# Sixteen element-wise transfers in DRAM in place of sixteen TensorE transposes of the key weights

## The chip, the cores and the metric

The kernel runs on one core of one Trainium2 chip. The metric is the device time of one execution in microseconds (us), lower is better. Engines are named as in the profile: PE is TensorE's matmul stream, PEld its weight loads, DVE is VectorE, ACT ScalarE, POOL GpSimd and SP SyncE. SP computes nothing: it issues transfers. A "q" behind an engine's name (SPq, ACTq) is that engine's sequencer, on which the issue of a transfer shows.

## The reference, cut to what matters

One decoder layer: RMSNorm, one input projection whose columns are split between two groups, an output projection with residual, and a last RMSNorm. Group A is a gated linear recurrence (eight blocks of 128 channels). Group B is attention with a small indexer that keeps 256 keys for each query. Its keys live in a shared latent `c` of 256 channels, and each of 8 heads has its own key weights `w_uk`:

```python
q_abs = jnp.einsum('bshd,hdc->bshc', q, w_uk)          # w_uk: 8 heads x 128 (d) x 256 (c), float32
...
logits = jnp.einsum('bqhc,bqkc->bqhk', qa_b, c_sel).astype(jnp.float32) * (HEAD_DIM ** -0.5)
```

The kernel uses the same product the other way: it makes each head's keys from the latent, keys = (w_uk turned) x c. For that TensorE needs `w_uk` with c, not d, over the 128 partitions: sixteen blocks (8 heads x 2 halves of c) of 128x128 float32 numbers, each turned. All of them together are 1 MB, 262,144 numbers.

## The kernel before, in words

Nearly every product is made in split precision: a float32 matrix is cut into a high and a low part and three matmuls are added (low x high, high x low, high x high). The program is written by hand for each engine, with semaphores, and each engine runs its own list strictly in order.

The stages are: loading and normalising x (turned by TensorE); tiles 0 to 2 of the input projection; the indexer, tiles 3 to 10; the recurrent stage, tiles 11 to 26, two for each of its eight blocks g; the attention's projections, tiles 27 to 42, two for each head h; the attention; the output projection.

A tile t of the projection goes in four pieces j. SP loads piece `w_raw` (256 KB) once the piece before it in the same place is used up (semaphore `w_lo_s`), POOL scales it (L809), ACT cuts the high part `w_hi` (function `high`, L903, which waits for PE to be done with the old piece, `w_used`), POOL makes the low part `w_lo` (L811), and PE runs 24 matmuls on it (`project_tile`, L1211 to L1213). There is one buffer per piece, so while PE works on piece j of tile t, piece j - 1 of tile t + 1 is made.

In the recurrent stage ACT's list for block g is (function `lru`): the two tiles' pieces, the first tap of the convolution `xc` (L1009), the high part of the gate weights (L1013), `xc_hi` (L1015), four pieces of the next tile, then the sigmoids, exp and root on the gates. PE's list is: both tiles, then `pe.wait_ge(gates_lo_s, g + 1)` and twelve matmuls of the gates (L1358 to L1360) on `xc_hi` and on `xc_lo`, which DVE makes (L1747). The first block's part of ACT's list begins after the indexer's last score (`ix_acc`).

The key weights: after the last recurrent block and the loads of tiles 27 and 28, SP loads `wuk` (L617, 1 MB, d over the partitions). PE turns it in sixteen transposes (L1376) after tile 28 and leaves the result in PSUM (`X[0]`, `X[1]`). ACT cuts the high parts (L1062), DVE the low ones (L1785), SP stores both to DRAM (L626), from where the attention loads each head's pair. Behind `wuk` on SP's list stand the stores of the last recurrent block (L594, L596) and the weights of the next tiles (L528).

Of the kernel before, what the change touches and what calls it, by code (L numbers as in the profile page):

```python
# [22 lines left out]
F32 = mybir.dt.float32  # L23
# [3 lines left out]
ACT = mybir.ActivationFunctionType  # L27
# [3 lines left out]
P = 128  # L31
# [5 lines left out]
G = LRU // P  # L37
CONV = 4
NH = 8
HD = 128  # L40
PAIRS = NH // 2
C = 256
CT = C // P
# [78 lines left out]
def layer(nc, a, out):  # L122
# [5 lines left out]
    ql_d = nc.dram_tensor("q_lo_dram", [NH, P, S], F32).ap()  # L128
    gate_d = nc.dram_tensor("gate_dram", [NH, P, S], F32).ap()
    c_d = nc.dram_tensor("c_dram", [CT, P, S], F32).ap()  # L130
    wkh_d = nc.dram_tensor("wuk_hi_dram", [NH, P, CT, HD], F32).ap()
    wkl_d = nc.dram_tensor("wuk_lo_dram", [NH, P, CT, HD], F32).ap()
    wvh_d = nc.dram_tensor("wuv_hi_dram", [PAIRS, P, CT, 2, HD], F32).ap()
# [5 lines left out]
    with ctx:  # L139
        def sem(name):  # L140
            return ctx.enter_context(nc.semaphore(name))

        def alloc(stack):
            return lambda name, shape, dt=F32: stack.enter_context(nc.sbuf_tensor(name, shape, dt))
# [11 lines left out]
        ident = sb("ident", [P, P])  # L156
# [44 lines left out]
        pu = ExitStack()  # L201
# [4 lines left out]
        pu = ExitStack()  # L206
# [3 lines left out]
        pu = ExitStack()  # L210
        cs_hi = alloc(pu)("cs_hi", [P, S], F32R)
        pu.close()
        pu = ExitStack()
# [17 lines left out]
        pu = ExitStack()  # L231
        y_hi = alloc(pu)("y_hi", [P, S], F32R)
        pu.close()
        pu = ExitStack()
# [3 lines left out]
        pu = ExitStack()  # L238
        xc_lo = alloc(pu)("xc_lo", [P, S], F32R)
        pu.close()  # L240
        pu = ExitStack()
# [4 lines left out]
        pu = ExitStack()  # L246
# [4 lines left out]
        pu = ExitStack()  # L251
        wuv = alloc(pu)("wuv", [P, PAIRS, CT, 2, HD])
        pu.close()
        pu = ExitStack()
# [3 lines left out]
        pu = ExitStack()  # L258
# [3 lines left out]
        pu = ExitStack()  # L262
# [3 lines left out]
        w_gates = sC("w_gates", [P, 2, P])  # L266
        mask_at = 4 * (3 * PIECES * PK * P + SCORED + 6 * S + 2 * P)
        pu = ExitStack()
        wuk = alloc(pu)("wuk", [P, NH, C])
        pu.close()  # L270
        pu = ExitStack()
        sU = alloc(pu)
# [3 lines left out]
        pu = ExitStack()  # L276
        wuv_hi = alloc(pu)("wuv_hi", [P, PAIRS, CT, 2, HD], F32R)
        pu.close()
        wuk_hi, wuk_lo = [wk0_hi, wk1_hi], [wk0_lo, wk1_lo]
# [10 lines left out]
        pu = ExitStack()  # L290
# [54 lines left out]
        PJ, X = PS[0:2], PS[2:4]  # L345
# [19 lines left out]
        bias_cp = sem("bias_cp")  # L365
        bias_st = sem("bias_st")
        wuk_in = sem("wuk_in")
        wuk_tp = sem("wuk_tp")
        wuk_hi_s = sem("wuk_hi_s")
        wuk_lo_s = sem("wuk_lo_s")  # L370
        wuk_st = [sem("wuk_st0"), sem("wuk_st1")]
# [58 lines left out]
        i_sig = sem("i_sig")  # L430
# [92 lines left out]
        def _(sp):  # L523
# [68 lines left out]
            def y_stores(g):  # L592
                sp.wait_ge(y_hi_s, g + 1)
                sp.dma_start(yh_d[ds(g, 1)].rearrange("o p s -> (o p) s"), y_hi[:, :].bitcast(F32)).then_inc(y_hi_st, 16)  # L594
                sp.wait_ge(y_lo_s, g + 1)
                sp.dma_start(yl_d[ds(g, 1)].rearrange("o p s -> (o p) s"), y_lo[:, :].bitcast(F32)).then_inc(y_lo_st, 16)  # L596
# [6 lines left out]
            def att_loads(h):  # L603
                weights(T_ATT + 2 * h, COL_Q + h * P)
                weights(T_ATT + 1 + 2 * h, COL_GB + h * P)
# [8 lines left out]
                sp.dma_start(gate_d[ds(h, 1)].rearrange("o p s -> (o p) s"), ig[:, :]).then_inc(gate_st, 16)  # L614

            att_loads(0)
            sp.dma_start(wuk[:, :, :], a["w_uk"][0].rearrange("h d c -> d h c")).then_inc(wuk_in, 16)  # L617
            y_stores(G - 1)

            att_loads(1)  # L620
# [244 lines left out]
        def _(act):  # L865
# [32 lines left out]
            def high(t, js=range(PIECES)):  # L898

                for j in js:  # L900
                    act.wait_ge(w_g_s, 4 * t + j - 3)
                    act.wait_ge(w_used, 4 * t + j + 1)
                    nc.scalar.activation(w_hi[:, j, :, :], w_raw[:, j, :, :], ACT.Copy).then_inc(w_hi_s, 1)  # L903
# [94 lines left out]
            def high_y(g):  # L998
                act.wait_ge(y_lru, g + 2)
                nc.scalar.activation(y_hi[:, :], sg[:, :], ACT.Copy).then_inc(y_hi_s, 1)  # L1000

            def lru(g, first=False):
                par = lambda k: lru_p[:, k, ds(g, 1)]
                if not first:
                    high(g * 2 + (T_LRU + 1), range(2))
                    high_y(g - 1)
                    high(g * 2 + (T_LRU + 1), range(2, PIECES))
                act.wait_ge(w_used, g * 8 + done(T_LRU))
                nc.scalar.activation(xc[:, :], PJ[1][:, :], ACT.Identity, scale=conv_w[:, CONV - 1, ds(g, 1)],  # L1009
                                     bias=par(0)).then_inc(xc0, 1)  # L1010

                act.wait_ge(gw_in, g * 32 + 32)
                nc.scalar.activation(wg_hi[:, :, :], w_gates[:, :, :], ACT.Copy).then_inc(wg_hi_s, 1)  # L1013
                act.wait_ge(pj_free[1], g + T_LRU // 2 + 2)
                nc.scalar.activation(xc_hi[:, :], xc[:, :], ACT.Copy).then_inc(xc_hi_s, 1)  # L1015
                high(g * 2 + (T_LRU + 2))
                act.wait_ge(gates_mm, g + 2)
                act.wait_ge(y_hi_st, 16 * g + 16)
                nc.scalar.activation(rg[:, :], X[0][:, :], ACT.Sigmoid, bias=par(1)).then_inc(r_sig, 1)
                nc.scalar.activation(ig[:, :], X[1][:, :], ACT.Sigmoid, bias=par(2)).then_inc(i_sig, 1)  # L1020
                act.wait_ge(y_lo_st, 16 * g + 16)
                nc.scalar.activation(sg[:, :], PJ[0][:, :], ACT.Sigmoid).then_inc(g_sig, 1)
                act.wait_ge(r_sig, g + 1)

                nc.scalar.activation(th[:, :], rg[:, :], ACT.Tanh, scale=decay[:, 0, ds(g, 1)])
                s = step.did(nc.scalar.activation(av[:, :], rg[:, :], ACT.Exp, scale=decay[:, 1, ds(g, 1)]))
                act.wait_ge(act_step, s)
                nc.scalar.activation(rg[:, :], av[:, :], ACT.Square).then_inc(a_sq, 1)
                act.wait_ge(one_m, g + 1)
                nc.scalar.activation(th[:, :], th[:, :], ACT.Sqrt).then_inc(root, 1)  # L1030

            lru(0, first=True)
            with act.Fori(1, G) as g:
                step.enter(g - 1, 1)
# [23 lines left out]

            att(0, first=True)
            for k in range(2):  # L1060
                act.wait_ge(wuk_tp, 2)
                nc.scalar.activation(wuk_hi[k][:, :, :], X[k][:, :].rearrange("p (t d) -> p t d", d=HD), ACT.Copy  # L1062
                                     ).then_inc(wuk_hi_s, 1)
            att(1)
            act.wait_ge(wuv_in, 16 * NH)
# [125 lines left out]
        def _(pe):  # L1191
# [88 lines left out]
            for n in range(2):  # L1280
                last = nc.tensor.matmul(X[0][0:ID, n * NT:(n + 1) * NT], ones_k[:, :],
                                        ks[:, n * NT:(n + 1) * NT], start=True, stop=True)
# [23 lines left out]
            for q in range(QB):  # L1306
                last = nc.tensor.transpose(X[0][:, q * IH:(q + 1) * IH], kw_sb[ID:KW, q * P:(q + 1) * P],
                                           ident[ID:KW, ID:KW])
# [59 lines left out]
            project_tile(T_ATT, 1, T_ATT // 2)  # L1368
            project_tile(T_ATT + 1, 0, (T_ATT + 1) // 2)

            pe.wait_ge(wuk_in, 16)
            pe.wait_ge(i_sig, G + 1)
            for k in range(2):
                for n in range(8):
                    h, t = (8 * k + n) // CT, n % CT
                    last = nc.tensor.transpose(X[k][:, n * P:(n + 1) * P], wuk[:, h, t * P:(t + 1) * P], ident[:, :])  # L1376
                last.then_inc(wuk_tp, 1)
            with pe.Fori(1, NH) as h:
                project_tile(h * 2 + T_ATT, 1, h + T_ATT // 2)
                project_tile(h * 2 + (T_ATT + 1), 0, h + (T_ATT + 1) // 2)  # L1380
# [159 lines left out]
            for q in range(HALF_T):  # L1540
                pe.wait_ge(o_add, 4 * (CHUNKS - 1) + q + 1)
                for kt in range(KT):
# [7 lines left out]
                    last = nc.tensor.matmul(o, hT_hi[:, kt, tok], whi, start=False, stop=(kt == KT - 1))  # L1550
# [4 lines left out]
        def _(dve):  # L1555
# [6 lines left out]
            tt, stt = nc.vector.tensor_tensor, nc.vector.scalar_tensor_tensor  # L1562
# [200 lines left out]
            def finish_gate(h):  # L1763
                dve.wait_ge(d_sig, h + 1)
                tt(ig[:, :], PJ[0][:, :], ig[:, :], ALU.mult).then_inc(pj_free[0], 1)

            def low_q(h):
                dve.wait_ge(q_hi_s, h + 1)
                dve.wait_ge(q_lo_st, h * 16 + 16)
                stt(q_out_lo[:, :], PJ[1][:, :], -HD ** -0.5, q_out_hi[:, :].bitcast(F32), ALU.mult, ALU.subtract  # L1770
                    ).then_inc(pj_free[1], 1)
# [3 lines left out]
            for h in range(2):  # L1775
                if h == 0:
                    low_q(h)
                top_rounds(per)
                if h == 1:
                    low_q(h)  # L1780
                finish_gate(h)
                if h == 0:
                    for k in range(2):
                        dve.wait_ge(wuk_hi_s, k + 1)
                        tt(wuk_lo[k][:, :, :], X[k][:, :].rearrange("p (t d) -> p t d", d=HD),  # L1785
                           wuk_hi[k][:, :, :].bitcast(F32), ALU.subtract).then_inc(wuk_lo_s, 1)
                else:
                    dve.wait_ge(wuv_hi_s, 1)
                    tt(wuv_lo[:, :, :, :, :], wuv[:, :, :, :, :], wuv_hi[:, :, :, :, :].bitcast(F32), ALU.subtract
                       ).then_inc(wuv_lo_s, 1)  # L1790
# [198 lines left out]
```

## Time and profile before

| | |
|---|---|
| time, median of 3 runs | 1567.97 us (1567.81 to 1569.97) |
| profiled execution, its own time | 1569.89 us |
| its span, first to last instruction | 1567.9 us |
| PE busy | 1551.3 us, 99% of the span |
| PEld / DVE / ACT / POOL busy | 84% / 56% / 37% / 41% |
| share of PE in the chain that ended last | 97% |
| mean granted TensorE clock | 0.997 of full |
| DMA packets | 142528 of 163.54 MB |

The chain that ended last is followed back from the last instruction, at each step to what released it; an engine's share of it says how much of the span that engine alone accounts for. The profiled execution is 1.9 us above the median, 0.12%; sums below are made against its 1569.9 us.

### The profile page before, as it was taken

How to read it: one execution, taken by the hardware profiler on the slowest of the kernel's cores; microseconds unless marked ns; L12 is line 12 of the kernel's file. 1: busy time of each engine (PE TensorE's matmuls, PEld its weight loads, DVE VectorE, ACT ScalarE, POOL GpSimd, SP SyncE). 2: the span in 40 equal slices, each digit the busy share in tenths (PEclk: the TensorE clock that was granted, in tenths of full speed). 3: DMA queues.
4: the chain of work that ended last, by engine and by line, in shares of the span. 5: the costliest groups of instructions: out<-in, count | busy, mean ns of one | idle time of the engine just before them, and what ended most of it. 6: DMA issues, size and time to landing. Idle time of an engine off the chain costs nothing.

```text
span 1567.9 us, 20944 instructions
## 1 busy us (share of the span) xinstructions
PE 1551.3 (99%) x7512; PEld 1324.1 (84%) x7512; DVE 870.3 (56%) x1516; ACT 581.5 (37%) x833; POOL 642.7 (41%) x461
## 2 busy tenths in 40 slices
PE   8999999999999999999999999999999999999997
PEld 7789999888888888888888888888888888888886
DVE  5477556588777887778654444577877000040003
ACT  7345555443344443342211111165655122222320
POOL 4354444435545445654444444200002444444640
PEclk9999999999999999999999999999999999999999
DMA  7222111022221222235422222244434623246422
GB/s 268 80 53 75 41 41 46 21 61 84 68 69 45 73 80 84 75 98 169 161 88 92 87 87 86 91 155 142 139 106 155 228 97 104 95 149 254 139 76 107
DMA packets 142528, 163.54 MB, mean 104 GB/s; under 512 B 9494, under 2 KB 106888, under 8 KB 140424
## 3 DMA queue, kind: packets, MB, share of 16 engines
q1 hardware_dynamic: 140936, 158.59, 31.3%
q0 software_dynamic: 1536, 4.20, 0.8%
q8 instruction: 36, 0.59, 0.2%
q14 instruction: 20, 0.16, 0.0%
HBM read 126.58 MB, written 36.18 MB: 104 GB/s over the span
## 4 chain that ended last, share of the span: by engine, by line
PE 97%; DVE 1%; DMA 0%; issue 0%; ACT 0%; DVEq 0%; SPq 0%
PE ps L1211 19%; PE ps L1212 19%; PE ps L1213 19%; PE ps L1462 6%; PE ps L1463 6%; PE ps L1461 6%; PE ps L1448 4%; PE ps L1332 2%; PE ps L1330 2%; PE ps L1429 2%; PE ps L1421 1%; PE ps L1423 1%; PE ps L1223 1%; PE ps L1422 1%; PE ps L1549 1%; PE ps L1548 1%
## 5 line engine op out<-in xcount | busy, mean ns | idle before, releaser
L1211 PE MATMUL ps<-hT_hi,w_lo 128*128 128x512 f32 (+1 forms) x1344 | 509.8, 379 | 0.0
L1213 PE MATMUL ps<-hT_hi,w_hi 128*128 128x512 f32 (+1 forms) x1344 | 509.1, 379 | 0.0
L1212 PE MATMUL ps<-hT_lo,w_hi 128*128 128x512 f32 (+1 forms) x1344 | 509.0, 379 | 0.0
L811 POOL TENSOR_TENSOR w_lo<-w_raw,w_hi 128x512 fp32r<-128x512 f32 x168 | 236.8, 1409 | 480.5 <-ACT w_hi L903 480.5
L1211 PEld LDWEIGHTS ps<-hT_hi,w_lo 128*128 128x128 f32 x1344 | 252.3, 188 | 43.4
L1212 PEld LDWEIGHTS ps<-hT_lo,w_hi 128*128 128x128 f32 x1344 | 252.4, 188 | 42.9
L1213 PEld LDWEIGHTS ps<-hT_hi,w_hi 128*128 128x128 f32 x1344 | 252.3, 188 | 42.8
L903 ACT ACTIVATE w_hi<-w_raw 128x512 fp32r<-128x512 f32 x168 | 106.0, 631 | 434.1 <-PE ps L1213 305.9
L809 POOL TENSOR_TENSOR w_raw<-w_raw,g_col 128x512 f32<-128x512 f32 x168 | 206.7, 1230 | 37.7 <-DMA w_raw<-in_w_in 37.7
L1928 DVE TENSOR_TENSOR res<-ps,res 128x512 f32<-128x512 f32 x32 | 21.9, 691 | 289.6 <-PE ps L1463 239.0
L839 POOL TENSOR_TENSOR wo_lo<-wo_raw,wo_hi 128x1024 fp32r<-128x1024 f32 x48 | 116.2, 2421 | 143.3 <-ACT wo_hi L1103 143.3
L1461 PE MATMUL ps<-wo_hi,hT_lo 128*128 128x512 f32 x448 | 174.5, 390 | 0.0
L1463 PE MATMUL ps<-wo_hi,hT_hi 128*128 128x512 f32 x448 | 174.3, 389 | 0.0
L1462 PE MATMUL ps<-wo_lo,hT_hi 128*128 128x512 f32 x448 | 174.3, 389 | 0.0
L1727 DVE MATCH_REPLACE8 scores<-top,scores 128x384 f32<-128x384 f32 (+2 forms) x192 | 165.7, 876 | 0.0
L1722 DVE MAX8 top<-scores 128x8 f32<-128x384 f32 (+2 forms) x192 | 155.3, 878 | 0.7
L1697 DVE SCALAR_TENSOR_TENSOR scores<-relu,w_nat,scores 128x384 f32<-128x384 f32 (+2 forms) x96 | 101.5, 1065 | 78.9 <-ACT relu L978 78.8
L1103 ACT ACTIVATE wo_hi<-wo_raw 128x1024 fp32r<-128x1024 f32 x48 | 50.9, 1060 | 185.1 <-PE ps L1463 185.1
L978 ACT ACTIVATE relu<-ps 128x384 f32<-128x384 f32 (+2 forms) x96 | 72.9, 760 | 72.9 <-PE ps L1332 64.7
L1461 PEld LDWEIGHTS ps<-wo_hi,hT_lo 128*128 128x128 f32 x448 | 84.1, 188 | 17.5
L1463 PEld LDWEIGHTS ps<-wo_hi,hT_hi 128*128 128x128 f32 x448 | 84.1, 188 | 17.4
L1462 PEld LDWEIGHTS ps<-wo_lo,hT_hi 128*128 128x128 f32 x448 | 84.1, 188 | 17.3
(217 smaller groups left out, 1908.0 us busy)
## 6 DMA issues: line engine op xcount, KB each, us to landing
w_raw<-in_w_in SPq DMA_DIRECT2D x168, 256.0 KB, 2.8
wo_raw<-in_w_out SPq DMA_DIRECT2D x64, 512.0 KB, 3.6
xin<-in_x SPq DMA_DIRECT2D x8, 1024.0 KB, 6.8
res<-in_x SPq DMA_DIRECT2D x8, 1024.0 KB, 11.3
out<-res SPq DMA_DIRECT2D x16, 512.0 KB, 4.0
y_hi_dram<-y_hi SPq DMA_DIRECT2D x8, 512.0 KB, 2.6
y_lo_dram<-y_lo SPq DMA_DIRECT2D x8, 512.0 KB, 2.7
q_hi_dram<-q_out_hi SPq DMA_DIRECT2D x8, 512.0 KB, 3.7
```

Of the source, the lines that this page charges most:

```text
L809: nc.gpsimd.tensor_tensor(part, part, gain(j, P), ALU.mult).then_inc(w_g_s, 1)
L811: nc.gpsimd.tensor_tensor(w_lo[:, j, :, :], part, w_hi[:, j, :, :].bitcast(F32), ALU.subtract).then_inc(w_lo_s, 1)
L839: nc.gpsimd.tensor_tensor(wo_lo[j % 2][:, :, :], wo_raw[j % 4], wo_hi[j % 2][:, :, :].bitcast(F32), ALU.subtract).then_inc(wo_lo_s, 1)
L903: nc.scalar.activation(w_hi[:, j, :, :], w_raw[:, j, :, :], ACT.Copy).then_inc(w_hi_s, 1)
L1211: nc.tensor.matmul(o, wlo, hi, start=(kt == 0), stop=False)
L1212: nc.tensor.matmul(o, whi, lo, start=False, stop=False)
L1213: return nc.tensor.matmul(o, whi, hi, start=False, stop=(kt == KT - 1))
L1461: nc.tensor.matmul(o, hT_lo[:, kt, tok], whi, start=(kt == 0), stop=False)
L1462: nc.tensor.matmul(o, hT_hi[:, kt, tok], wlo, start=False, stop=False)
L1463: last = nc.tensor.matmul(o, hT_hi[:, kt, tok], whi, start=False, stop=(kt == KT - 1))
L1722: found = step.did(nc.vector.max(top8[:, q, :], scores[:, off(q):off(q) + (q + 1) * P]))
L1727: marked = step.did(nc.vector.match_replace(left, top8[:, q, :], left, TAKEN))
```

## The change

SP no longer loads `w_uk` for TensorE to turn. ACT issues sixteen transfers from `w_uk` to a new DRAM tensor `wkt_d`, one for each head and half of c, at the start of the recurrent stage, ahead of the first block's `xc`. Each reads one block with d and c exchanged, so that runs that lie next to each other in the destination (512 B over d) are 128 numbers that lie 1 KB apart in the source: it moves 16,384 single float32 numbers. SP waits for all sixteen (`wuk_turned`) before it loads the turned weights into `wuk`. PE's transposes are gone; ACT and DVE cut `wuk` from SBUF in place of PSUM. The second half's high part is written over the first half of `wuk`, so ACT waits there for DVE's first low part.

```diff
+    wkt_d = nc.dram_tensor("wuk_turned_dram", [P, NH * CT, HD], F32).ap()
...
-        wuk = alloc(pu)("wuk", [P, NH, C])
+        wuk = alloc(pu)("wuk", [P, NH * CT, HD])
...
             att_loads(0)
-            sp.dma_start(wuk[:, :, :], a["w_uk"][0].rearrange("h d c -> d h c")).then_inc(wuk_in, 16)
+            sp.wait_ge(wuk_turned, 16 * NH * CT)
+            sp.dma_start(wuk[:, :, :], wkt_d[:, :, :]).then_inc(wuk_in, 16)
             y_stores(G - 1)
...
+            for h in range(NH):
+                for t in range(CT):
+                    act.dma_start(wkt_d[:, h * CT + t, :], a["w_uk"][0, h, :, t * P:(t + 1) * P].rearrange("d c -> c d"), allow_slow_non_contiguous=True
+                                  ).then_inc(wuk_turned, 16)
             lru(0, first=True)
...
             att(0, first=True)
             for k in range(2):
-                act.wait_ge(wuk_tp, 2)
-                nc.scalar.activation(wuk_hi[k][:, :, :], X[k][:, :].rearrange("p (t d) -> p t d", d=HD), ACT.Copy
+                act.wait_ge(wuk_in, 16)
+                if k == 1:
+                    act.wait_ge(wuk_lo_s, 1)
+                nc.scalar.activation(wuk_hi[k][:, :, :], wuk[:, 8 * k:8 * k + 8, :], ACT.Copy
                                      ).then_inc(wuk_hi_s, 1)
...
-            pe.wait_ge(wuk_in, 16)
-            pe.wait_ge(i_sig, G + 1)
-            for k in range(2):
-                for n in range(8):
-                    h, t = (8 * k + n) // CT, n % CT
-                    last = nc.tensor.transpose(X[k][:, n * P:(n + 1) * P], wuk[:, h, t * P:(t + 1) * P], ident[:, :])
-                last.then_inc(wuk_tp, 1)
...
-                        tt(wuk_lo[k][:, :, :], X[k][:, :].rearrange("p (t d) -> p t d", d=HD),
+                        tt(wuk_lo[k][:, :, :], wuk[:, 8 * k:8 * k + 8, :],
                            wuk_hi[k][:, :, :].bitcast(F32), ALU.subtract).then_inc(wuk_lo_s, 1)
```

ACT's list where the recurrent stage begins, before (L903 is `w_hi`, L1009 `xc`, L1013 the gate weights, L1015 `xc_hi`):

```order
L978 ACTIVATE relu<-ps 128x1024 [waits ix_acc,ix_mm]
L903 ACTIVATE w_hi<-w_raw 128x512 [waits w_used,w_g_s]
L1009 ACTIVATE xc<-ps,par_t 128x1024 [waits w_used,dec_s,ix_acc]
L1013 ACTIVATE wg_hi<-w_gates 128x256 [waits gw_in]
L1015 ACTIVATE xc_hi<-xc 128x1024 [waits pj_free1]
```

The same place in the changed kernel, where line numbers are 2 higher:

```order
L980 ACTIVATE relu<-ps 128x1024 [waits ix_acc,ix_mm]
L905 ACTIVATE w_hi<-w_raw 128x512 [waits w_used,w_g_s]
L1036 DMA wuk_turned_dram<-in_w_uk 128x128x1 [waits dec_s,ix_acc]
L1036 DMA wuk_turned_dram<-in_w_uk 128x128x1 x15
L1011 ACTIVATE xc<-ps,par_t 128x1024 [waits w_used]
L1015 ACTIVATE wg_hi<-w_gates 128x256 [waits gw_in]
L1017 ACTIVATE xc_hi<-xc 128x1024 [waits pj_free1]
```

Sixteen issues now stand between the indexer's last work on ACT and the recurrent stage's first, and they took over `xc`'s waits.

SP's list from the loads of tiles 27 and 28 (the x8), before:

```order
L528 DMA w_raw<-in_w_in 128x4x128 [waits w_lo_s] x8
L617 DMA wuk<-in_w_uk 128x8x256
L594 DMA y_hi_dram<-y_hi 128x1024 [waits y_hi_s]
L596 DMA y_lo_dram<-y_lo 128x1024 [waits y_lo_s]
L528 DMA w_raw<-in_w_in 128x4x128 [waits w_lo_s] x8
```

And in the changed kernel:

```order
L529 DMA w_raw<-in_w_in 128x4x128 [waits w_lo_s] x8
L619 DMA wuk<-wuk_turned_dram 128x2048 [waits wuk_turned]
L595 DMA y_hi_dram<-y_hi 128x1024 [waits y_hi_s]
L597 DMA y_lo_dram<-y_lo 128x1024 [waits y_lo_s]
L529 DMA w_raw<-in_w_in 128x4x128 [waits w_lo_s] x8
```

The load of `wuk` stands where it stood, and now waits for the sixteen transfers, with two stores and eight weight pieces behind it.

## Rows read from the trace of the kernel before

**Rows 1.** The page: busy time of each engine, and the chain that ended last.

```profile
PE 1551.3 (99%) x7512; PEld 1324.1 (84%) x7512; DVE 870.3 (56%) x1516; ACT 581.5 (37%) x833; POOL 642.7 (41%) x461
...
PE 97%; DVE 1%; DMA 0%; issue 0%; ACT 0%; DVEq 0%; SPq 0%
```

**Rows 2.** Timeline of PE around the transposes: start us, us, engine, line, operation.

```profile
708.49 0.39 PE L1213 MATMUL ps<-hT_hi,w_hi 128*128 128x512 f32 x1
708.72 1.91 PE L1376 MATMUL ps<-ident,wuk 128*128 128x128 f32 x16
710.39 0.48 PE L1211 MATMUL ps<-hT_hi,w_lo 128*128 128x512 f32 x1
710.70 0.39 PE L1212 MATMUL ps<-hT_lo,w_hi 128*128 128x512 f32 x1
```

**Rows 3.** Timeline of SP from 1400 to 1413 us: transfers issued.

```profile
1401.79 8.64 SPq L738 DMA_DIRECT2D out<-res  x8
```

**Rows 4.** The issues of L738 between 1400 and 1413 us: duration ns min/median/max.

```profile
L738 SPq DMA_DIRECT2D out<-res x8: 430/1178/1484, 1401.8 to 1409.2; - x8
```

**Rows 5.** DMA from 1403 to 1410 us: packets, MB, share of 16 engines.

```profile
DMA packets 817, 2.62 MB, mean 375 GB/s; under 512 B 72, under 2 KB 72, under 8 KB 817
...
q1 hardware_dynamic: 817, 2.62, 101.0%
```

**Rows 6.** DMA from 336.5 to 339 us, one `w_raw` piece.

```profile
DMA packets 528, 0.26 MB, mean 105 GB/s; under 512 B 16, under 2 KB 528, under 8 KB 528
...
q1 hardware_dynamic: 528, 0.26, 38.5%
```

**Rows 7.** DMA from 410.96 to 411.16 us.

```profile
DMA packets 16, 0.00 MB, mean 0 GB/s; under 512 B 16, under 2 KB 16, under 8 KB 16
...
q1 hardware_dynamic: 16, 0.00, 4.5%
```

**Rows 8.** DMA from 10.7 to 12.7 us, rows of 320 B of the first tile.

```profile
DMA packets 1824, 0.57 MB, mean 283 GB/s; under 512 B 1824, under 2 KB 1824, under 8 KB 1824
...
q1 hardware_dynamic: 1824, 0.57, 119.9%
```

**Rows 9.** Timelines of ACT, DVE and PE where the recurrent stage begins.

```profile
317.30 0.63 ACT L903 ACTIVATE w_hi<-w_raw 128x512 fp32r<-128x512 f32 x1 [0.39 <-PE ps L1213]
318.26 1.21 ACT L1009 ACTIVATE xc<-ps,par_t 128x1024 f32<-128x1024 f32 x1 [0.33 <-DVE scores L1697]
...
324.89 1.23 DVE L1747 TENSOR_TENSOR xc_lo<-xc,xc_hi 128x1024 fp32r<-128x1024 f32 x1 [0.79 <-ACT xc_hi L1015]
...
338.80 0.39 PE L1358 MATMUL ps<-xc_hi,wg_lo 128*128 128x512 f32 x1
```

**Rows 10.** Busy time, granted clock and DMA share from the stage's start to `wuk`'s load.

```profile
318.20:665.10 346.90, 346.90 (x1532) 287.36 (x1531) 270.95 (x396) 142.26 (x161) 178.30 (x129) 1.00 0.24 72
```

**Rows 11.** Timeline of SP: the load of `wuk`, the stores and weights behind it.

```profile
665.13 0.51 SPq L617 DMA_DIRECT2D wuk<-in_w_uk  x1
690.61 0.36 SPq L594 DMA_DIRECT2D y_hi_dram<-y_hi  x1
693.38 0.36 SPq L596 DMA_DIRECT2D y_lo_dram<-y_lo  x1
693.79 17.58 SPq L528 DMA_DIRECT2D w_raw<-in_w_in  x8
```

**Rows 12.** The page's DMA issues: KB each, median us from issue to landing.

```profile
wuk<-in_w_uk SPq DMA_DIRECT2D x1, 1024.0 KB, 5.4
```

**Rows 13.** Timelines of ACT and DVE where `wuk` is cut.

```profile
711.85 1.94 ACT L1062 ACTIVATE wk_hi<-ps 128x1024 fp32r<-128x1024 f32 x2
716.21 0.63 ACT L903 ACTIVATE w_hi<-w_raw 128x512 fp32r<-128x512 f32 x1 [2.42 <-PE ps L1213]
721.64 0.63 ACT L903 ACTIVATE w_hi<-w_raw 128x512 fp32r<-128x512 f32 x1 [4.81 <-PE ps L1213]
...
716.21 2.35 DVE L1785 TENSOR_TENSOR wk_lo<-ps,wk_hi 128x1024 fp32r<-128x1024 f32 x2
```

More of the change, by code:

```diff
@@ L367, in layer @@
         wuk_in = sem("wuk_in")
-        wuk_tp = sem("wuk_tp")
+        wuk_turned = sem("wuk_turned")
         wuk_hi_s = sem("wuk_hi_s")
```

## The prediction

> **What bounds the kernel now.** I read the page's busy times and its chain first: PE is busy 1551.3 of 1567.9 us and makes 97% of the chain that ended last [rows 1]. So work taken off PE is worth its own time, and whatever leaves PE without operands costs its full length. Then I read PE's timeline at the transposes, ACT, DVE and PE at the start of the recurrent stage, SP at the load of `wuk`, and last the DMA counters of short stretches for the price of a packet. The question is one of two places: the 1.7 us at 708 us that the change gives back, and the sixteen issues at 318 us with which it pays.
>
> **What it removes.** PE starts the first transpose at 708.72 and the next matmul at 710.39 [rows 2], 1.67 us apart. The matmul after that one starts 0.31 us later, while other matmuls stand 0.23 us apart, so 0.08 us more hang on the turn-over. The gain is 1.67 to 1.75 us; I take 1.7 us, 0.11% of 1569.9. That is the most the change can bring, since nothing else leaves PE. It lies below the 0.2% that I take a measurement of this kernel to tell from no change.
>
> **What it adds: the number of packets.** A piece of `w_raw` is 256 KB in source runs of 512 B, and the stretch with one such piece has 528 packets, 512 of them of 512 B or more and 16 small ones [rows 6]: one packet for each contiguous run. A turned block has runs of one number, so I count 128 x 128 = 16,384 packets per transfer and 262,144 for all sixteen, against 142,528 in the whole kernel before. Over 16 DMA engines that is 16,384 packets on each.
>
> **The price of a packet.** No row has a 4-byte number read from and written to DRAM. Three rows surround it. Sixteen packets of under 512 B and together under 0.01 MB took 4.5% of 16 engines x 200 ns = 144 ns, 9.0 ns each [rows 7]: small, but not 16,384 of them in a row and perhaps no data at all. Packets of 320 B: 119.9% of 16 x 2000 ns over 1,824 packets, 21.0 ns each [rows 8]. Packets of 512 B beside little else: 38.5% of 16 x 2500 ns over 528, 29.2 ns each [rows 6]. By the first the sixteen transfers last T = 16,384 x 9.0 ns = 147 us, by the second 344 us, by the third 478 us. Numbers that lie next to each other in the destination come in separate packets, and no row shows what such a write costs in DRAM, so as an upper end I take twice the third, 58.4 ns and 957 us. I take 21.0 ns, the row nearest to a short run that is data read from DRAM; it lies between the ends. T = 344 us.
>
> The Trainium skill says in "DMA: Bandwidth & Descriptors", Rules for kernel authors, that a strided last dimension is lowered to one descriptor per element and should be rearranged away. The trace agrees with what one can see of it, one packet to a run of 512 B [rows 6].
>
> **Who waits while they drain.** The row that decides is SP at 1401.79 us: eight stores of 512 KB issued back to back take 8.64 us [rows 3], with a median of 1.18 us and a minimum of 0.43 us for an issue [rows 4]. Over these 7 us the 16 DMA engines were full (101%), at 375 GB/s [rows 5]; 524,288 B at 375 GB/s is 1.40 us, near the 1.18 us of an issue. So once a few transfers are outstanding, an issue doesn't finish before earlier packets have gone, and the issuing engine runs at the pace of the DMA engines. There it was held with a few hundred packets ahead of it. One element-wise transfer has 16,384. I therefore expect ACT to stand in these sixteen issues for nearly all of T: only what the queue takes, a few hundred packets of 262,144, is left when ACT goes on.
>
> Behind them on ACT stand `xc`, the gate weights, `xc_hi` and every later `w_hi` [rows 9]. Nothing covers that for long. When ACT would begin `xc` at 318.26, the last piece of tile 12 has just been cut (317.30), so PE has work until the gates' matmuls at 338.80 [rows 9]: 20.5 us. From `xc`'s start to the end of DVE's `xc_lo`, which the gates wait for, it takes 324.89 + 1.23 - 318.26 = 7.9 us [rows 9]. PE thus stands for T - 20.5 + 7.9 = T - 12.6 us. After that the pieces of tile 13 come one by one behind `xc_hi`, but POOL has scaled them while ACT stood and twelve gate matmuls run first; I cost this at nothing, at most some 3 us.
>
> The Trainium skill has the same step in "Perfetto Trace Analysis", DMA Instruction — HWDGE: the generator is locked until all descriptors of a transfer are made, and the sequencer is free only afterwards. Taken with the rows above it speaks against the change; the sum doesn't need it.
>
> **What it moves.** SP now waits at 665.13 for all sixteen transfers. If ACT is held, they are nearly done when it goes on, so this wait costs nothing; if ACT is not held, it is the place to look (below). The load itself moves the same 1 MB in longer runs, so I leave it at its 5.4 us [rows 12]. At the cut, ACT's second high part now waits for DVE's first low part: DVE begins it at 716.21 and needs 1.2 us, ACT's second part ends near 718.5 instead of 713.8 [rows 13]. Behind it stands a `w_hi` that ran at 716.21; it comes 2.3 us later. The next stood idle 4.81 us before it [rows 13], which takes that up, and PE reaches the piece some three pieces later, so it costs nothing. Without that cover it would be 2.3 us.
>
> **Sum**, against the profiled 1569.9 us: + 344 - 12.6 - 1.7 = 1569.9 + 329.7 = 1899.6, about **1900 us**. The median of the runs shown lies 1.9 us lower, which doesn't matter at this size.
>
> **Rivals.**
>
> *A. Hidden (not slower).* The queue takes each transfer's description at once, ACT is free after sixteen cheap issues, and the packets drain beside the recurrent stage. For it: the DMA engines are 24% busy from 318.2 to 665.1, PE has all its operands there [rows 10], and single issues of other transfers take 0.34 to 0.51 us (SP's row for `wuk`, 1 MB: 0.51 us [rows 11]), 16 of them 8 us against 12.6 us of cover. Against it: rows 3 to 5. It decides at T below 665.1 - 318.2 = 346.9 us [rows 10], 21.2 ns for a packet. Price: 1569.9 - 1.7 = 1568.2 us. I give it 0.07.
>
> *B. Hidden on ACT, late on SP.* As A, but with T above 346.9 us. SP stands at the load of `wuk`, and behind it wait the two stores (690.61, 693.38) and the weights of tile 29 (693.79) [rows 11], so up to 28.7 us of this wait are free and PE stands for T - 346.9 - 28.7 and what the pieces need: with 478 us, + 102 us, 1670 us. 0.03.
>
> *C. Held, but the packets are cheap.* At 9.0 ns: 1569.9 + 147 - 14.3 = 1703 us. The forecast's mechanism with the lower price; 0.20.
>
> *D. Held, and DRAM makes single numbers dear.* From 30 to 58 ns: 1569.9 + 492 - 14 = 2048 to 1569.9 + 957 - 14 = 2513 us; above that, more. 0.27 for 30 to 58 ns and 0.10 for above.
>
> *E. One rule, another price.* A transfer of 1 MB done nineteen times slower than `wuk`'s own load of 5.4 us [rows 12] takes 103 us, and with ACT held that gives 1569.9 + 103 - 14.3 = 1659 us. That would be 6.3 ns for a packet, less than any row has; 0.04. The Trainium skill says in "VectorE: DVE Perf Modes", in the table of transpose paths, that a plain copy with strides is 19 times slower than the hardware's transposing one; no run here has that one.
>
> That leaves 0.29 for the forecast with a price of some 12 to 30 ns, 1750 to 2050 us; it is the likeliest single case.
>
> **How the numbers follow.** ACT held (the forecast, C, D, E) has 0.90, B 0.03, A 0.07. Slower by over 0.2% is all of these but A: 0.93. A is within 0.2%: 0.06 to 0.07. Faster by over 0.2% needs a gain of 3.1 us where 1.7 us are to be had: 0.01. The range goes from just below E and B, 1650 us, to D's upper end, 2515 us. It leaves out A (0.07), what lies above 58 ns (0.10) and B with a T near its threshold (0.01), 0.18 together.
>
> **What the changed kernel's profile would show.** Sixteen issues on ACTq from 318 us, each long: with the forecast some 21 us, with A under 1 us. PE idle from 339 us until 8 us after ACT's last issue, released by ACT and DVE (`xc_hi`, `xc_lo`). The packet count up by 262,144, all under 512 B, and DMA engines near full for T. SP without a long wait at `wuk`. No transposes at the end of tile 28, and 1.7 us less from there to the end. Wrong it would be if ACT's issues are short, if the packets aren't one for each number, or if a number costs far from 21 ns; the first changes the sign, the others only the size.

## The result, and the profile after

The changed kernel takes 6470.35 us in the median of 4 runs (6414.12 to 6527.18), against 1567.94 us of the kernel before in the same comparison. The ratio is 4.113, with a 95% interval of 4.105 to 4.121; it is made of the fast executions' means and leaves out the one of 6527.18 us, which counts as slow. The profiled execution took 6414.12 us, with a span of 6412.2 us. The forecast was 1900 us in a range of 1650 to 2515 us.

The page of the changed kernel: busy times, the clock in 40 slices, DMA queues, the chain that ended last (it answers to [rows 1]).

```profile
PE 1569.2 (24%) x7496; PEld 1333.8 (21%) x7496; DVE 868.4 (14%) x1516; ACT 581.3 (9%) x833; POOL 639.7 (10%) x461
...
PEclk9955555555555555555555555555555569999999
...
DMA packets 404032, 164.59 MB, mean 26 GB/s; under 512 B 271894, under 2 KB 368264, under 8 KB 401800
...
q10 hardware_dynamic: 262400, 1.05, 113.1%
q1 hardware_dynamic: 140040, 158.59, 11.2%
...
issue 79%; PE 18%; POOL 2%; DVE 0%; DMA 0%; ACT 0%; POOLq 0%; SPq 0%; DVEq 0%; ACTq 0%
```

PE has as much work as before and spends 76% of a span four times as long without any. The transfers have a queue of their own, q10, with 262,400 packets for 1.05 MB: one for each of the 262,144 numbers, and 256 more. "Issue", the chain's 79%, is time in which an engine waited for nothing that the profile ascribes to a releaser.

The sixteen issues on ACT (duration ns min/median/max), then ACT's timeline, then the chain of waits (us in total, times, longest):

```profile
L1036 ACTq DMA_DIRECT2D wuk_turned_dram<-in_w_uk x16: 708/292722/341838, 318.3 to 4514.1; - x16
```

```profile
317.29 0.63 ACT L905 ACTIVATE w_hi<-w_raw 128x512 fp32r<-128x512 f32 x1 [0.39 <-PE ps L1221]
318.25 4529.33 ACTq L1036 DMA_DIRECT2D wuk_turned_dram<-in_w_uk  x16
4847.64 1.20 ACT L1011 ACTIVATE xc<-ps,par_t 128x1024 f32<-128x1024 f32 x1 [4529.71 <-issue]
```

```profile
PE ps L1366 <- DVE xc_lo L1748: 4580.3, 2, 4516.6
ACT xc L1011 <- issue: 4529.7, 1, 4529.7
POOL w_raw L811 <- DMA w_raw<-in_w_in: 479.4, 17, 166.6
...
PE ps L1219 <- POOL w_lo L813: 243.3, 6, 150.1
```

The first issue took 0.7 us; the median of all sixteen is 292.7 us, and the other fifteen have a mean of 302 us ((4529.3 - 0.7) / 15). ACT began `xc` at 4847.64 where it had begun at 318.26 [rows 9], 4529.4 us later, and PE's one wait for `xc_lo` lasted 4516.6 us: 12.8 us less, where 12.6 us of cover were counted.

The same stretches by engine (from, to, length; busy of PE, PEld, DVE, ACT, POOL; granted clock; DMA share, GB/s):

```profile
338.80:4855.40 4516.60, 0.15 (x1) 0.00 (x0) 5.32 (x6) 3.08 (x4) 1.62 (x2) 0.50 1.55 0
4855.40:5260.00 404.60, 94.48 (x332) 73.48 (x333) 64.55 (x100) 35.11 (x39) 37.54 (x29) 0.60 1.15 11
5260.00:6412.20 1152.20, 1142.71 (x5365) 958.34 (x5363) 608.34 (x1214) 377.92 (x571) 454.69 (x315) 1.00 0.35 116
```

The span grew by 6412.2 - 1567.9 = 4844.3 us. The first row holds 4516.6 of it. The second holds 404.6 - 94.5 = 310.1 us more in which PE had nothing, although ACT was free. PE's own busy time grew by 17.9 us (1569.2 against 1551.3) although 1.9 us of transposes are gone: after 4516 us without work the granted clock stood at 0.50, the lower of its two levels (1.2 GHz), and it was 1.00 again only once PE was fed. Together that is 4844.6 us. The third row runs as before.

What starved PE in the second row shows in POOL's timeline and in the DMA counters from ACT's release to 5260 us:

```profile
4864.41 1.30 POOL L813 TENSOR_TENSOR w_lo<-w_raw,w_hi 128x512 fp32r<-128x512 f32 x1 [0.74 <-ACT w_hi L905]
5032.31 1.04 POOL L811 TENSOR_TENSOR w_raw<-w_raw,g_col 128x512 f32<-128x512 f32 x1 [166.59 <-DMA w_raw<-in_w_in]
```

```profile
q10 hardware_dynamic: 16641, 0.07, 74.2%
q1 hardware_dynamic: 7200, 4.46, 38.8%
```

A whole transfer was still to drain when ACT went on: 16,641 packets, of which 16,400 are its own (16,384 numbers and 16 more) and 241 the rest of the one before. The weight pieces were loaded beside it. While POOL waited, from 4865 to 5032 us, the counters were:

```profile
q10 hardware_dynamic: 8883, 0.04, 110.7%
q1 hardware_dynamic: 2113, 1.04, 42.2%
```

A packet of the weights' queue q1 is recorded with 42.2% of 16 x 167 us / 2,113 = 534 ns here, against 29.2 ns in the same reckoning before [rows 6].

### The profile page after: what moved, and what is told of

It reads as the page before. It is cut to its first block, busy times and chain, and to the rows that moved or that the text cites. A ratio compares the mean times of both kernels' runs of the same rounds, so it can differ in the third digit from the quotient of the medians.

```text
span 6412.2 us, 20928 instructions
## 1 busy us (share of the span) xinstructions
PE 1569.2 (24%) x7496; PEld 1333.8 (21%) x7496; DVE 868.4 (14%) x1516; ACT 581.3 (9%) x833; POOL 639.7 (10%) x461
## 3 DMA queue, kind: packets, MB, share of 16 engines
q10 hardware_dynamic: 262400, 1.05, 113.1%
## 4 chain that ended last, share of the span: by engine, by line
issue 79%; PE 18%; POOL 2%; DVE 0%; DMA 0%; ACT 0%; POOLq 0%; SPq 0%; DVEq 0%; ACTq 0%
PE ps L1219 3%; PE ps L1220 3%; PE ps L1221 3%; PE ps L1464 2%; PE ps L1463 2%; PE ps L1462 2%; POOL w_raw L811 1%; POOL w_lo L813 1%; PE ps L1449 1%; PE ps L1430 0%; PE ps L1422 0%; PE ps L1424 0%; PE ps L1423 0%; PE ps L1550 0%; PE ps L1551 0%
## 5 line engine op out<-in xcount | busy, mean ns | idle before, releaser
L1366 PE MATMUL ps<-xc_hi,wg_lo 128*128 128x512 f32 x32 | 14.5, 452 | 4580.3 <-DVE xc_lo L1748 4580.3
L813 POOL TENSOR_TENSOR w_lo<-w_raw,w_hi 128x512 fp32r<-128x512 f32 x168 | 235.7, 1403 | 4885.9 <-ACT w_hi L905 4885.9
L1738 DVE SCALAR_TENSOR_TENSOR xc<-ps,par_t,xc 128x1023 f32<-128x1023 f32 (+2 forms) x24 | 30.8, 1282 | 4749.6 <-ACT xc L1011 4747.3
```

The source lines that it names most:

```text
L813: nc.gpsimd.tensor_tensor(w_lo[:, j, :, :], part, w_hi[:, j, :, :].bitcast(F32), ALU.subtract).then_inc(w_lo_s, 1)
```

## The experiments

All kernels but e7 keep the place of the sixteen issues. Two theories stood at the start. W: writing single numbers into DRAM is what costs (about 290 us for a transfer's 1,024 packets on each of 16 DMA engines). R: reading single numbers 1 KB apart is. e3 and e7 were run eleven times each; the others once each, so that a small difference between two of them (28.0 us a transfer in e8 against 33.7 in e4) isn't read.

**e1_sbuf.** The transfers write into `wuk` itself, in SBUF; SP loads nothing.

```diff
-                    act.dma_start(wkt_d[:, h * CT + t, :], a["w_uk"][0, h, :, t * P:(t + 1) * P].rearrange("d c -> c d"), allow_slow_non_contiguous=True
-                                  ).then_inc(wuk_turned, 16)
+                    act.dma_start(wuk[:, h * CT + t, :], a["w_uk"][0, h, :, t * P:(t + 1) * P].rearrange("d c -> c d"), allow_slow_non_contiguous=True
+                                  ).then_inc(wuk_in, 16)
```

> The sixteen turning transfers write into SBUF (the buffer that the attention cuts) in place of DRAM; same source runs of one number, same count of packets, no load by SP. Theory W (the 299 ns per number and engine are the price of writing single numbers into DRAM): a packet falls to the 9 to 30 ns of the rows of before, ACT is held 150 to 490 us, about 1700 to 2050 us in all. Theory R (the price is that of reading single numbers 1 KB apart in DRAM): nothing changes, ACT held some 4500 us, about 6400 us. Theory B (both sides share it): in between.

Measured: 1705.84 us. The issues (duration ns min/median/max) and ACT's timeline:

```profile
L1034 ACTq DMA_DIRECT2D wuk<-in_w_uk x16: 442/9762/12337, 318.0 to 455.6; - x16
```

```profile
318.04 147.58 ACTq L1034 DMA_DIRECT2D wuk<-in_w_uk  x16
465.68 1.20 ACT L1009 ACTIVATE xc<-ps,par_t 128x1024 f32<-128x1024 f32 x1 [147.96 <-issue]
```

The same reads, the same 262,400 packets, and a transfer takes 9.76 us in place of 292.7: 9.5 ns for each packet of a DMA engine. R is refuted; the price is on the write side, and it is thirty times that of SBUF. ACT was held all the same, 148.0 us.

**e2_strided_writes.** The loops of a transfer are exchanged: it reads the source in its own order and writes each number 8 KB from the last.

```diff
+                    act.dma_start(wkt_d[:, h * CT + t, :].rearrange("c d -> d c"), a["w_uk"][0, h, :, t * P:(t + 1) * P], allow_slow_non_contiguous=True
```

> The same numbers turned with the loops exchanged: the source is read in its own order, neighbouring numbers after each other, and each is written alone, 8 KB from the last; output unchanged, 262,144 packets as before. Theory W, if any lone write is dear: as the changed kernel, about 6400 us; if only writes next to each other in one line are dear: well under 2500 us. Theory R: reads of neighbours are cheap, so under 2500 us.

Measured: 2961.88 us.

```profile
L1036 ACTq DMA_DIRECT2D wuk_turned_dram<-in_w_uk x16: 710/89877/99631, 316.0 to 1576.5; - x16
```

Less than a third of the price (89.9 us a transfer) with the same writes in another order, but above the 2500 us that the expectation had named for cheap writes, so no branch of it came true. e8 below asks what makes the rest.

**e4_apart.** As the changed kernel, but the destination has 64 B for each number. SP loads `wuk` from its source, after the wait.

```diff
-    wkt_d = nc.dram_tensor("wuk_turned_dram", [P, NH * CT, HD], F32).ap()
+    wkt_d = nc.dram_tensor("wuk_turned_dram", [P, NH * CT, HD, 16], F32).ap()
...
+                    act.dma_start(wkt_d[:, h * CT + t, :, 0], a["w_uk"][0, h, :, t * P:(t + 1) * P].rearrange("d c -> c d"), allow_slow_non_contiguous=True
```

> As the changed kernel, but each number is written 64 B from the next, so that no two writes that follow each other touch the same 64 B; SP loads the weights unturned from their source after the wait (that part of the computation is wrong, the transfers are all there). Theory W with neighbours in one line as the cause: a packet falls under 100 ns, total under 3200 us. Theory W with any lone write dear, or theory R: about 6400 us.

Measured: 2067.8 us.

```profile
L1036 ACTq DMA_DIRECT2D wuk_turned_dram<-in_w_uk x16: 710/33660/38705, 317.4 to 789.7; - x16
```

33.7 us a transfer, 33 ns a packet. So a lone write into DRAM costs some three and a half times one into SBUF, and the step from there to 286 ns comes with writes close to each other. The counters of q10 from 360 to 780 us, while ACT stood:

```profile
q10 hardware_dynamic: 205422, 0.82, 42.2%
```

By the count, a packet takes 16 x 420 us / 205,422 = 32.7 ns of a DMA engine, in agreement with the issues. By the share of recorded packet time, which is how the prediction priced its rows, it would be 42.2% of that, 13.8 ns. In the changed kernel the share is too high instead: 113.1% of 16 x 6412.2 us over 262,400 packets is 442 ns by the page, where the issues give 286 ns.

**e8_apart_swapped.** e2's order with e4's spacing.

```diff
+                    act.dma_start(wkt_d[:, h * CT + t, :, 0].rearrange("c d -> d c"), a["w_uk"][0, h, :, t * P:(t + 1) * P], allow_slow_non_contiguous=True
```

> As e2_strided_writes (source read in its own order), but each number has 64 B of the destination to itself, so that no two engines write in the same 64 B at about the same time; SP loads the weights unturned (that part of the computation is wrong, the transfers are all there). If the 86 us of a transfer in e2_strided_writes against the 33 us of e4_apart came from neighbours in one 64 B that two engines or near packets write: 33 us or less for each, about 2060 us. If they came from writes that are far apart (a step of many KB): 86 us or more, 2900 us or more.

Measured: 1972.24 us.

```profile
L1036 ACTq DMA_DIRECT2D wuk_turned_dram<-in_w_uk x16: 710/27990/30176, 316.3 to 703.5; - x16
```

28.0 us against e2's 89.9 (which the expectation puts at 86): neighbours cost even when their writes don't follow each other directly, and a large step between writes, here 128 KB, is not dear.

**e9_apart_32 and e10_apart_8.** e4's destination with 32 B (e9, shown) and with 8 B (e10, a last dimension of 2) for each number.

```diff
-    wkt_d = nc.dram_tensor("wuk_turned_dram", [P, NH * CT, HD, 16], F32).ap()
+    wkt_d = nc.dram_tensor("wuk_turned_dram", [P, NH * CT, HD, 8], F32).ap()
```

> As e4_apart with 32 B in place of 64 B between written numbers (weights loaded unturned, that part of the computation is wrong). If the price comes with following writes in the same 32 B, a transfer takes 33 us as in e4_apart, about 2070 us in all. If the same 64 B count, two neighbours meet and it takes clearly more, 45 us or more, over 2260 us.

> As e4_apart with 8 B between written numbers, eight of them in 64 B and four in 32 B (weights loaded unturned, that part of the computation is wrong). If writes in one line wait for each other one by one, nearly all of them still do, and a transfer takes close to the 303 us of the changed kernel, over 5000 us in all. If the price grows evenly with how many share a line, it falls to about half, some 150 us for each and 4000 us in all.

Measured: 2311.37 and 3961.35 us. The issues of e9, then of e10:

```profile
L1036 ACTq DMA_DIRECT2D wuk_turned_dram<-in_w_uk x16: 710/48590/57938, 316.1 to 1005.6; - x16
```

```profile
L1036 ACTq DMA_DIRECT2D wuk_turned_dram<-in_w_uk x16: 710/149922/157528, 318.2 to 2434.5; - x16
```

| written numbers in 64 B | median of an issue, us | per packet of a DMA engine, ns (issue / 1,024) |
|---|---|---|
| 1 (e4) | 33.7 | 33 |
| 2 (e9) | 48.6 | 47 |
| 8 (e10) | 149.9 | 146 |
| 16 (changed kernel) | 292.7 | 286 |

The price lies near a line, 15 ns and 17 ns for each number written in the same 64 B (15 + 17 x 16 = 287). That two numbers 32 B apart still meet speaks for a unit of at least 64 B. A larger one isn't excluded: the spacing thins the writes in 128 B or 512 B in the same proportion, so the four prices would lie on a line by that count too, and it also spreads them over up to sixteen times the memory. Counting by 64 B is a choice; what is shown is that the price grows with how densely the numbers are written.

**e6_last_turned.** Fifteen straight copies, and only the last transfer turned, in DRAM. Nothing stands behind it on ACT.

```diff
+                    part = a["w_uk"][0, h, :, t * P:(t + 1) * P]
+                    if h == NH - 1 and t == CT - 1:
+                        part = part.rearrange("d c -> c d")
+                    act.dma_start(wkt_d[:, h * CT + t, :], part, allow_slow_non_contiguous=True).then_inc(wuk_turned, 16)
```

> Fifteen of the sixteen transfers are straight copies in runs of 512 B, the last alone is turned, in DRAM as in the changed kernel (the other fifteen blocks of key weights aren't turned, so that part of the computation is wrong). Nothing is issued on ACT behind it, so ACT isn't held. Theory H (the loss is ACT's holding alone): 1566 us. Theory S (the weight loads also suffer while single numbers drain into DRAM, as behind the last transfer of the changed kernel, where PE lost some 300 us though ACT was free): 1566 us and some 250 to 300 us, about 1840 us, with POOL waiting for w_raw.

Measured: 1824.98 us. ACT's timeline, SP's, and the waits:

```profile
318.37 10.66 ACTq L1039 DMA_DIRECT2D wuk_turned_dram<-in_w_uk  x16
329.08 1.21 ACT L1011 ACTIVATE xc<-ps,par_t 128x1024 f32<-128x1024 f32 x1 [11.04 <-PE ps L1223]
```

```profile
319.57 50.91 SPq L529 DMA_DIRECT2D w_raw<-in_w_in  x8
373.63 94.64 SPq L585 DMA_DIRECT2D w_gates<-in_lru_wa  x1
```

```profile
POOL w_raw L811 <- DMA w_raw<-in_w_in: 311.8, 16, 147.4
...
PE ps L1221 <- POOL w_lo L813: 223.2, 4, 118.1
```

Theory S holds, and not H: holding ACT costs nothing here (16 issues in 10.7 us, inside its cover), and the kernel still loses 259 us to one transfer (against e3 below). SP's own issue of 64 KB took 94.64 us, and POOL waited up to 147.4 us for a weight piece. The loads of the changed kernel behind ACT's release show the same. So there are two losses: ACT held behind a transfer, and SP's loads beside it.

**e3_straight.** All sixteen copy straight, in runs of 512 B.

```diff
+                    act.dma_start(wkt_d[:, h * CT + t, :], a["w_uk"][0, h, :, t * P:(t + 1) * P]).then_inc(wuk_turned, 16)
```

> The sixteen transfers copy their blocks without turning them (runs of 512 B on both sides, 2,048 packets in all; the kernel then uses key weights that aren't turned, so this part of the computation is wrong). All theories: ACT is held by 16 cheap issues of 0.4 to 1.2 us, hidden in the 12.6 us of cover; what is left is the change without its element-wise side. I expect 1.7 us less than before, 1566 us, within 0.2%.

Measured: 1566.22 us (11 runs) against 1568.89, ratio 0.9988, interval 0.9979 to 0.9997. The issues:

```profile
L1036 ACTq DMA_DIRECT2D wuk_turned_dram<-in_w_uk x16: 605/619/831, 316.1 to 326.0; - x16
```

The bytes, the place on ACT, SP's wait and the new waits at the cut cost nothing. What the change could bring is this.

**e7_sbuf_spread.** e1's transfers, two in each recurrent block, so that each has drained before the next.

```diff
+            def turn(h, t):
+                act.dma_start(wuk[:, ds(h * CT + t, 1), :].rearrange("c o d -> c (o d)"),
+                              a["w_uk"][0, ds(h, 1), :, t * P:(t + 1) * P].rearrange("o d c -> c (o d)"),
+                              allow_slow_non_contiguous=True).then_inc(wuk_in, 16)
...
                 nc.scalar.activation(xc_hi[:, :], xc[:, :], ACT.Copy).then_inc(xc_hi_s, 1)
+                turn(g, 0)
...
                 nc.scalar.activation(th[:, :], th[:, :], ACT.Sqrt).then_inc(root, 1)
+                turn(g, 1)
```

> As e1_sbuf, into SBUF, but two issues in each of the eight recurrent blocks, one behind xc_hi and one behind the block's last root, some 20 us apart. A transfer took 9.8 us in e1_sbuf, so each has drained when the next is issued. If ACT is held only when an earlier transfer is outstanding: sixteen issues of some 0.45 us in ACT's idle time, no transposes and no load by SP, 1566 us, level with e3_straight and within 0.2% of before. If a lone turning transfer also holds or starves the weight pieces: slower than before by up to 16 x 10 us.

Measured: 1567.13 us (11 runs) against 1569.03, ratio 0.9988, interval 0.9979 to 0.9997. The issues, and the DMA queues while one transfer drains (349 to 366 us):

```profile
L1035 ACTq DMA_DIRECT2D wuk<-in_w_uk x16: 388/388/442, 322.9 to 675.1; - x16
```

```profile
q10 hardware_dynamic: 16400, 0.07, 83.8%
q1 hardware_dynamic: 144, 0.52, 7.5%
```

262,400 element packets, all turned, and every issue takes 0.39 us: both losses are gone when each transfer is short and the last one has drained. It is 1.9 us faster than the kernel before (0.5 to 3.3 us by the interval), which agrees with the 1.7 us counted for the transposes and with e3: this is what the change can give here.

## Why the prediction was wrong

Its direction and the holding of ACT behind its transfers held. One term of its sum, the price of a packet, was too small by a factor of some fourteen, and a second, put at nothing, was 310 us.

*What bounds the kernel, and the gain.* Right. Without the transposes the kernel is some 2 us faster (e3, e7), where 1.7 us were counted.

*One packet for each number.* Right: 262,400 on q10.

*The price of a packet.* This is the step that failed: "I take 21.0 ns, the row nearest to a short run that is data read from DRAM", with "twice the third, 58.4 ns" as upper end. Measured are 286 ns a packet by the median issue, 295 ns by the mean of the fifteen long ones. No row that the prediction reads has single numbers written next to each other in DRAM, and it is that closeness that made 286 ns of 33 (the changed kernel against e4). I had named this write ("no row shows what such a write costs in DRAM") and bounded it from above all the same, by doubling; the outcome lies in the part of case D above 58 ns, which had a chance of 0.10 and was left out of the range. The way in which the rows were priced was unsafe too: the share of recorded packet time isn't the pace of the packets, as e4 shows (13.8 ns by the share, 32.7 ns by the count). That the 9.0 ns row comes near e1 (9.5 ns) and the 29.2 ns row near e4 (33 ns) is then partly luck. With 302 us for each of the fifteen transfers that held ACT, in place of 21.5, the same sum holds: the measured stretch on ACT, 4529.3 us, less the cover gives 4516.7 us, and PE's wait was 4516.6.

*ACT held.* Right, and the cover of 12.6 us too (12.8 us). Case A (hidden) is refuted by the sixteen long issues, and its other half, that a single outstanding transfer costs nothing, by e6, for DRAM. With packets of 9.5 ns and one transfer at a time it is what happens (e7).

*"Only what the queue takes, a few hundred packets, is left when ACT goes on."* Wrong. A whole transfer was left, 16,641 packets, and the first issue, with nothing ahead of it, took 0.7 us. An issue of these transfers waits until the one before it has all but drained (241 packets of 16,400 were left of it at the end of the last issue), not for its own packets.

*The pieces behind it "at nothing, at most some 3 us".* Wrong, and the second step that failed: 310 us, because that last transfer drained beside the loads of `w_raw`, whose packets are recorded with 534 ns in place of 29.2 ns. e6 shows it alone (259 us). The size of this term follows from the first error: at 9.5 ns a packet (e1) the same rest is 10 us and doesn't show.

*SP's wait at `wuk`, the cut.* Right, both cost nothing; e3 has both.

*Case C* (held, cheap packets: 1703 us) is e1 with 1705.84 us. The sum is sound at that price, but so close a hit has some luck in it: a packet took 9.5 ns and not 9.0, and ACT was held for fifteen transfers and not sixteen, which nearly cancel. Case E's 6.3 ns lies under the price in every run with element-wise transfers.

The clock was in no term. With the clock at 0.60 in the stretch after its wait, PE's own work was 19.8 us longer (17.9 + the 1.9 us of transposes that are gone).

What stays open: where the price of close writes is spent, in the memory or on the path to it, and how large the unit is in which they meet. The runs show that it grows with how densely the numbers are written, and that they need not follow each other (e2 against e8). Why an issue of SP's for 64 KB waits 94.64 us beside a single transfer of ACT (e6) isn't settled either: the profile counts both queues on the same 16 DMA engines, but no run separates those engines from the memory as the place where they meet.

## What to carry to other kernels

Count a rearranged transfer in packets, not in bytes, and price it by what it writes into as well: to turn a matrix of float32 by single numbers cost 9.5 ns a packet into SBUF and 286 ns into neighbouring addresses in DRAM. Issue such a transfer only from an engine that can stand still, or one at a time with its drain time before the next; beside a long one the other queue's loads suffered too (e6). Price packets by their count in a stretch where they are what limits, not by the share of recorded time. When the trace has no row for a cost, an upper bound that is made by doubling its nearest rows is a guess: let the range say so, and look first at what the change can win (here 1.7 us) before it is worth any risk.

## What the runs showed of the hardware

- The price of writing single float32 numbers into DRAM by how many fall into 64 B: 33, 47, 146 and 286 ns for 1, 2, 8 and 16 numbers (e4, e9, e10, the changed kernel). Into SBUF it was 9.5 ns (e1).
- The queue let one element-wise transfer through in 0.4 to 0.7 us and held the issuer of the next until the one before had all but drained: 9.8, 28, 34, 49, 90, 150 and 293 us, by the price of its packets. It isn't the number of transfers that holds: sixteen straight ones, 2,304 packets on q10 in all, were issued in 0.6 to 0.8 us each (e3).
- Reading single float32 numbers 1 KB apart in DRAM is not what costs: with SBUF as destination such a packet took 9.5 ns, read and write together (e1).
- The DMA share of the profile rose to 155% with PE waiting: the times of packets overlap. In e4 it was 42% while every issue waited for the packets before it. So the share is no measure of what is left of the DMA engines.
